# First products of the second and third block on unscaled tiles, residual on one engine, stick scores on all rows

## What is computed

```python
def _rmsnorm(a, gain):
    af = a.astype(jnp.float32)
    af = af * lax.rsqrt(jnp.mean(af * af, axis=-1, keepdims=True) + EPS)
    return (af * gain.astype(jnp.float32)).astype(a.dtype)
...
z = jnp.einsum('bqhd,bkhd->bhqk', qb.astype(jnp.float32), kf) * scale
...
h = rmsnorm_3(x, norm_mix_g[l])
z = h @ w_in[l]
```

## Time and profile before

| | us |
|---|---|
| runs: median of 3 | 2980.92 |
| runs: lowest, highest | 2980.76, 2983.86 |
| the profiled execution | 2986.45 |
| its span | 2984.7 |
| PE, DVE, ACT, POOL busy in it | 2856.8, 1363.2, 1138.4, 1227.8 |

### The profile page before, as it was taken

The page is one execution under the profiler, slowest core; times in us unless marked ns, Lnnn a source line. Parts: engine busy times, 40 slices in busy tenths (PEclk is TensorE's granted clock), DMA queues, the critical chain, the costliest instruction groups (busy, mean ns, idle before and its releaser), DMA issues. The chain is left out here.

```text
span 2984.7 us, 39962 instructions
## 1 busy us (share of the span) xinstructions
PE 2856.8 (96%) x16029; PEld 2324.9 (78%) x16029; DVE 1363.2 (46%) x2463; ACT 1138.4 (38%) x2061; POOL 1227.8 (41%) x590
## 2 busy tenths in 40 slices
PE   6999999999999979999999999999999999999998
PEld 4865558888988867767888989888787767888887
DVE  6336650341132332764553555632477653556620
ACT  4357762222244333333454422222333355422221
POOL 4432224454444532222223545554445423555553
PEclk9999999999999988989999999999999999999999
DMA  7410002223322211112323422223222223422332
GB/s 265 148 50 15 15 29 99 95 96 99 117 90 98 92 50 63 37 42 94 121 76 123 137 85 92 98 98 105 85 85 81 87 74 113 148 90 99 99 99 91
DMA packets 84088, 274.71 MB, mean 92 GB/s; under 512 B 9727, under 2 KB 9983, under 8 KB 83776
## 3 DMA queue, kind: packets, MB, share of 16 engines
q1 hardware_dynamic: 82568, 271.32, 27.6%
q10 hardware_dynamic: 1336, 0.83, 0.1%
HBM read 257.36 MB, written 17.90 MB: 92 GB/s over the span
## 5 line engine op out<-in xcount | busy, mean ns | idle before, releaser
L135 POOL TENSOR_TENSOR weights_lo<-weights_raw,weights_hi 128x1024 fp32r<-128x1024 f32 x413 | 1001.9, 2428 | 1330.4 <-ACT weights_hi L127 1330.4
L127 ACT ACTIVATE weights_hi<-weights_raw 128x1024 fp32r<-128x1024 f32 x413 | 436.3, 1060 | 1055.9 <-PE acc L494 543.4
L492 PE MATMUL acc<-h_hi,weights_hi 128*128 128x512 f32 (+2 forms) x1800 | 663.1, 368 | 25.2 <-POOL h_lo L1374 6.5
L493 PE MATMUL acc<-h_lo,weights_hi 128*128 128x512 f32 (+2 forms) x1800 | 637.5, 354 | 0.0
L494 PE MATMUL acc<-h_hi,weights_lo 128*128 128x512 f32 (+2 forms) x1800 | 637.3, 354 | 0.0
L492 PEld LDWEIGHTS acc<-h_hi,weights_hi 128*128 128x128 f32 x1800 | 344.7, 192 | 106.3 <-issue 53.9
L494 PEld LDWEIGHTS acc<-h_hi,weights_lo 128*128 128x128 f32 x1800 | 344.8, 192 | 46.1
L493 PEld LDWEIGHTS acc<-h_lo,weights_hi 128*128 128x128 f32 x1800 | 345.5, 192 | 40.8 <-issue 0.2
L538 PE MATMUL acc<-weights_hi,h_hi 128*128 128x256 f32 (+2 forms) x448 | 137.2, 306 | 11.9 <-DVE h_lo L1002 5.2
L830 ACT ACTIVATE probs<-probs,low 128x31 f32<-128x31 f32 (+5 forms) x276 | 139.1, 505 | 20.7 <-DVE low L797 20.2
L492 PE MATMUL acc<-y_hi,weights_hi 128*128 128x512 f32 (+1 forms) x384 | 137.9, 359 | 3.1 <-POOL y_lo L1693 2.7
(11 more groups left out here) (437 smaller groups left out, 5285.6 us busy)
## 6 DMA issues: line engine op xcount, KB each, us to landing
weights_raw<-in_stream SPq DMA_DIRECT2D x413, 512.0 KB, 3.3
weight_ring<-in_w_ada SPq DMA_DIRECT2D x24, 512.5 KB, 8.3
gates<-gate_tiles SPq DMA_DIRECT2D x24, 258.0 KB, 4.1
gate<-gates SPq DMA_DIRECT2D x8, 774.0 KB, 5.2
held<-gates SPq DMA_DIRECT2D x8, 768.0 KB, 5.7
gates<-gate_tiles SPq DMA_DIRECT2D x23, 256.0 KB, 4.1
bias_copies<-bias_rows SPq DMA_DIRECT2D x1, 3068.0 KB
table<-bias_copies SPq DMA_DIRECT2D x1, 2560.0 KB, 10.0
```

The costliest lines, as they stand in the source:

```text
L127: act.activation(self.hi[:, at % CUT, :], self.raw[:, at % RAW, :], ACT.Copy).then_inc(self.hi_done, 1)
L135: pool.tensor_tensor(self.lo[:, at % CUT, :], self.raw[:, at % RAW, :], self.hi[:, at % CUT, :].bitcast(F32), ALU.subtract).then_inc(self. ...
L492: pe.matmul(out, left[0], right[0], start=start, stop=False)
L493: pe.matmul(out, left[0], right[1], start=False, stop=False)
```

## The change

At the edge from the first to the second block the residual is added on DVE alone. The normalization behind it also makes unscaled halves of the eight tiles, the low half one tile behind on DVE, and a lane `Led` runs two weight chunks (the stick queries, four units, 32 triples) on these halves into four PSUM banks: 20 triples between the residual's tiles, 7 ahead of the `wide` product and 5 behind it. `ChunkAhead` does the load, the rounding and the low halves of one more chunk ahead of the root. In the second block four more chunks (64 triples) run on the unscaled halves; DVE multiplies their results by the scale as it takes them. `TakeLed` takes the led ones into `alone`, one head to a tile with zeros on the other 64 rows (`Blank`), and `Scaled` is spread on DVE between them. The stick scores then use all 128 rows. At the edge from the second to the third block two chunks (the convolution's values, 16 triples) are led in the same way, two triples ahead of the last sums, four ahead of the `wide` product, ten behind it, without a `ChunkAhead`; two chunks of the recurrence's heads follow on unscaled halves, then the led results are taken, then `Scaled` comes. The three runs become one that is renewed between the blocks with the same end, clearing and barrier. The weights lie in the new order of use.

```diff
@@ Run: one for the three blocks
+    def renew(self):
+        self.close()
+        self.open()
...
@@ new lane: the chunk after the led ones
+class ChunkAhead(Lane):
...
+    def sp(self, sp):
+        self.ws.load(sp, self.first, AHEAD + RAW)
...
+    def act(self, act):
+        self.ws.round(act, self.first, AHEAD)
...
+    def pool(self, pool):
+        self.ws.rest(pool, self.first, AHEAD)
...
+class TakeLed(Lane):
...
+    def dve(self, dve):
+        for u, take in enumerate(self.takes):
+            take(dve, self.acc[:, u]).then_inc(self.taken, 1)
+            yield
...
@@ Norm.dve
-            if self.cut is not None:
-                self.rest(dve, t).then_inc(self.lo_even if t % 2 == 0 else self.lo_odd, 1)
+            if self.cut is not None and t >= self.behind:
+                self.low(dve, t - self.behind)
...
         dve.tensor_scalar(self.root[:, 0], self.sums[0:4, 0:self.quarter], 1.0 / D, EPS, ALU.mult, ALU.add).then_inc(self.mean_done, 1)
+        if self.cut is not None and self.behind:
+            self.low(dve, KT - 1)
...
@@ Residual.dve
             dve.scalar_tensor_tensor(self.source(t), self.source(t), self.gain(t), self.scale, ALU.mult, ALU.mult).then_inc(self.scaled, 1)
-            if t % 2 == 0:
-                self.add(dve, t).then_inc(self.even, 1)
-            yield
-
-    def pool(self, pool):
-        for t in range(KT):
-            if t % 2 == 1:
-                self.add(pool, t).then_inc(self.odd, 1)
+            dve.wait_ge(self.scaled, t + 1)
+            dve.tensor_tensor(self.out(t), self.out(t), self.source(t), ALU.add).then_inc(self.added, 1)
             yield
@@ feed_forward, with a next norm
-                order = spliced(down.slots, [(t + 1) * down.per + 1 for t in range(KT)] + [down.slots] * 2)
-                run.lanes([0] * up.slots + [1 + lane for lane in order], [up, down, norm])
+                led = led_of.open(sem, psum, ws, norm.ready_unscaled)
+                order = [1 + lane for lane in spliced(down.slots, [(t + 1) * down.per + 1 for t in range(KT)])]
+                order += [3] * 2 + [2] + [3] * 4 + [2] + [3] * (led.slots - 6)
+                run.lanes([0] * up.slots + order, [up, down, norm, led])
...
+class Led:
...
+    def open(self, sem, psum, ws, ready):
+        units = [unit for c in range(self.chunks) for unit in feature_units(ws, c, self.source, self.n, self.w, ready=(lambda pe, t: ready(pe, t)) if c == 0 else None)]
+        self.dense = Dense(sem, psum, ws, units, self.chunks, banks=len(units), abreast=len(units), acc=self.acc, lags=self.lags, hold=self.hold)
+        return self.dense
@@ first_block, last phase
+                led_of = Led(lambda t: k.vec[:, gain + t:gain + t + 1], raw, N2, W2, LED2, lead, [1.5, 1.5, 5, 5], 1)
...
-                after = Norm(sem, sbuf, k, A, tiles_of(b.x, N2, W2), T2, N2, W2, added.ready, psum("sums", [P, 512]), psum("wide", [P, N2, 512]), b.scale[:, :])
-                lanes = [dense, cut, norm, added, after]
+                after = Norm(sem, sbuf, k, A, tiles_of(b.x, N2, W2), T2, N2, W2, added.ready, sums, wide, b.scale[:, :], cut=led_of.cut, behind=True)
+                led = led_of.open(sem, psum, ws, lambda pe, t: after.ready_unscaled(pe, t))
+                lanes = [dense, cut, norm, added, after, led, ChunkAhead(ws, led.first)]
...
-                run.lanes(order + [3, 4] * KT + [4] * 2, lanes, 2 * KT)
+                marks = led.marks()
+                tail = [step for t in range(KT) for step in [3, 4] + [5] * len([at for at in marks if t - 1 < at - 0.5 <= t])]
+                left = led.slots - tail.count(5)
+                run.lanes(order[:-1] + [6] + order[-1:] + tail + [4] + [5] * 7 + [4] + [5] * (left - 7), lanes, 2 * KT)
@@ Stick.pe, score
-            rows = slice((head % 2) * HD, (head % 2) * HD + HD)
...
-            pe.matmul(self.scores[0:ROWS2[kb], i % 2, 0:W2], self.fm[rows, SB_K + head // 2, kb * P:kb * P + ROWS2[kb]],
-                      self.qm[rows, SB_Q + head // 2, half * W2:(half + 1) * W2], start=True, stop=True).then_inc(self.scores_ready, 1)
+            pe.matmul(self.scores[0:ROWS2[kb], i % 2, 0:W2], self.fm[:, SB_K + head // 2, kb * P:kb * P + ROWS2[kb]],
+                      self.alone[:, head, half * W2:(half + 1) * W2], start=True, stop=True).then_inc(self.scores_ready, 1)
@@ second_attention, first phase
+            def heads_apart(i, half):
+                def take(dve, acc):
+                    cols = columns_of(half)
+                    dve.tensor_tensor(alone[0:HD, 2 * i, cols], acc[0:HD, 0:w], scale[0:HD, cols], ALU.mult)
+                    return dve.tensor_tensor(alone[HD:P, 2 * i + 1, cols], acc[HD:P, 0:w], scale[HD:P, cols], ALU.mult)
+                return take
+
+            def scaled_tile(dest, i):
+                return lambda dve, half, acc: dve.tensor_tensor(dest[:, i, columns_of(half)], acc, scale[:, columns_of(half)], ALU.mult)
...
-                units = token_units(ws, 0, h, T2, values(SB_V), ready=scaled.ready)
-                for i in range(SP_Q + 2):
-                    units += feature_units(ws, 2 + i, h, n, w, act=tile(qm, i))
...
+                for i in range(2):
+                    units += feature_units(ws, i, lambda t: raw.tile(t, T2), n, w, dve=scaled_tile(qm, SP_Q + i))
+                for i in range(2):
+                    units += feature_units(ws, 2 + i, lambda t: raw.tile(t, T2), n, w, dve=scaled_tile(early, SB_K + i))
...
+                others = [2] + [3] * takes.slots + [1] * scaled.slots
+                begin = 2 * KT
+                span = raw_slots - begin
+                order = [0] * begin
+                for at, lane in enumerate(others):
+                    order += [lane] + [0] * ((at + 1) * span // len(others) - at * span // len(others))
+                run.lanes(order + [0] * (dense.slots - raw_slots), [dense, scaled, apart, takes])
@@ second_block
+        led_of = Led(lambda t: k.vec[:, mix + t:mix + t + 1], next_raw, 1, S, LED3, next_lead, [0, 0], 0)
@@ third_mixer, first phase
-                units = feature_units(ws, 0, h, 1, S, act=tile(value, 0), ready=scaled.ready) + feature_units(ws, 1, h, 1, S, act=tile(value, 1))
...
+                raw_heads = 2
+                units = [unit for i in range(raw_heads) for unit in feature_units(ws, i, lambda t: raw.tile(t, S), 1, S, dve=scaled_tile(hf, i))]
...
+                takes = TakeLed(sem, next_lead, [lambda dve, acc, i=i: dve.tensor_tensor(value[:, i, :], acc, scale, ALU.mult) for i in range(LED3)])
...
-                order = paced((dense.weights, 0, 1), (convolved.weights, 0.16, 1), (decays.weights, 0.3, 0.8))
-                run.lanes([3] * scaled.slots + order, [dense, convolved, decays, scaled])
+                order = paced((dense.weights, 0, 1), (convolved.weights, 0.2, 1), (decays.weights, 0.3, 0.8))
+                run.lanes(order[:raw_slots] + [4] * takes.slots + [3] * scaled.slots + order[raw_slots:], [dense, convolved, decays, scaled, takes])
```

## The result

The changed kernel takes 2991.91 us, median of 6 runs, against 2981.87 for the kernel before: a ratio of 1.004 (95% interval 1.0027 to 1.0053). It is **slower**, by 0.4%: 12 us by the ratio, 10 between the medians. The forecast was 2966, faster by 14.5. The profiled execution took 2995.28, its span is 2993.5.

The account below looks back on a forecast made before the run. TensorE, busy 2856.8 of 2984.7 us (96%), was taken as the bound. Edge 1's 8, edge 2's 0.5 and the scores' 6 sum to 14.5 us off the median of 2980.92, giving 2966; range 2955 to 2977.

Parts of the forecast that it names:

- Everything else: Weight tile order, memory on the other side and renewed blocks, throughout the kernel: counts of barriers and loads unchanged, costing nothing.
- A: The forecast itself, whole kernel: 14.5 us faster, 2966 us, own range 2958 to 2975; chance 0.62.
- Edge 1: First block into second: led products gain 11.8 us, less 3.4 for late takes and 0.5 for low clock; about 8.
- The stalls: Second block's raw phase: three DVE operations beside POOL, standing in front of takes, delay products by 3.4 us, bounds 2 and 5.
- the clock: Edge 1: low clock on the first led triples, which stand among idle time, costs half a microsecond.
- Edge 2: Second block into third: a gain of 4.5 us less 4 us of stall, about +0.5, range -2 to +3.
- both stalls: Edge 2: PE idle 4.8 us at the block end behind a late chunk, then 4 us waiting on Scaled's low halves.
- Scores: Stick stage: 32 scores on 128 rows save up to 0.39 us each, 12.5 in all; half taken, 6.
- D: Rival: DVE bounds both opening phases, loss once its waits exceed 22 us; slower, 2990 us; chance 0.04.
- B: Rival: the stick scores give nothing, so the gain is 8.5 us, 2972.4; chance 0.14.
- C: Rival: edge 2's late chunk and Scaled are hidden, so the gain is 21.5 us, 2959.4; chance 0.12.
- E: Rival: at edge 1 the 20 led triples between residual tiles run late, gaining 7.3 us less, 2973.7; chance 0.08.

Follow-up runs that it names:

- b_before_off: The kernel before, with the normalized halves of the first and third block moved by 32 bytes, tile distance still 2048: 3003.65 us, ratio to before 1.0074.
- j_before_2112: The kernel before, with the first block's normalized halves 2112 bytes apart instead of 2048, start unchanged: 2988.03 us, ratio to before 1.0025.
- l_before_2176: The kernel before, with the first block's normalized halves 2176 bytes apart instead of 2048, start unchanged: 2987.80 us, ratio to before 1.0025.
- e_flat128: The changed kernel, with halves starting on a multiple of 128 bytes and the first block's tiles 2048 bytes apart: 2972.85 us, ratio to before 0.9969.
- k_scaled_dve: h_banks3 with all of Scaled's low halves on DVE, none on POOL: 2955.26 us, ratio to before 0.9917.
- g_scaled_first: e_flat128 with edge 2's two led units run one after the other, and its led takes and Scaled ahead of raw products: 2960.56 us, ratio 0.9933.
- h_banks3: g_scaled_first with three PSUM banks instead of two for dense units of the second block's first phase: 2959.13 us, ratio to before 0.9931.
- i_rows64: h_banks3 with the stick scores reading 64 rows again: 2963.06 us, ratio to before 0.9945.
- the two pairs: a_aligned and h_banks3, each against itself with 64-row scores: 2981.92 against 2989.12 us, and 2959.13 against 2963.06 us.
- a_aligned: The changed kernel with 32 bytes per partition reserved on the right side, so tensors there start on multiples of 64 bytes: 2981.92 us, ratio to before 1.0001.
- f_stride: The changed kernel with halves starting on a multiple of 128 bytes, the first block's tiles still 2112 bytes apart: 2983.32 us, ratio to before 1.0006.

## Why the prediction was wrong

**The step that failed** is the one that costed the rest of the edit: "Everything else (order of weight tiles, memory on the other side, renewed blocks) leaves counts of barriers and loads as they are: nothing." Counts did stay. But the memory on the other side moved the operands of the first and third block's products, and each product became 2 to 3% longer: 344 in 80 us instead of 354. It costs 12.6 us in the first block and 6.9 in the third block's rest. b_before_off, j_before_2112 and l_before_2176 show it in the kernel before, by place alone; e_flat128 takes it out of the change. The work before an edge was taken for unchanged because its code was. With the 19.5 of these two places in it, the forecast's sum would have been -5, a slower kernel; no rival named it. (A's own range, 2958 to 2975, is narrower than its three bounds added up, which give 2954 to 2979; the result lies outside both.)

**With that taken out** (e_flat128), the edit gives 0.31%, 9 us, where 14.5 were forecast. Term by term, from the table:

- *Edge 1*, forecast 8: 108.2 - 106.0 = 2.2 (3.2 in the changed kernel itself, on which the following stands). The stalls were priced well (3.4; one gap of 3.17 and one of 0.54), by the mechanism that was named. The mis-sized term is the clock, 0.5: behind the idle time of the block's end the window from 1100 shows 0.62, behind the gap that from 1128 shows 0.57, together (0.38 + 0.43) x 4 = 3.2 us. And the start was 1.6 later than worked out: when the last add ended (1085.99), eight led triples and the sums of the tile before were still ahead of the last sums on the PE, and not four triples, so these began at 1090.42 - 12.6 = 1077.8 instead of 1076.5. Clock 3.2 - 0.5 = 2.7, start 1.6 and stalls 3.7 - 3.4 = 0.3 make 4.6 of the 4.8 that are missing. Where the clock falls differs from trace to trace: in e_flat128 it is 1.00 behind the same idle time of 1.75 (window from 1091), but 0.50 from 1060 to 1064, among the led products, and from 1116 to 1120, behind the gap. k_scaled_dve, with three banks and no POOL in Scaled, has 108.2 - 99.2 = 9.0, with the full clock in its whole raw phase: the 8 could be reached, in part by luck with the clock.
- *Edge 2*, forecast 0.5: 521.3 - 521.2 = 0.1, in a column that varies by up to 4 between like kernels, so that the nearness says little. But both stalls stood where they were put, and both could be taken away: g_scaled_first gains 10.0 there, h_banks3 and i_rows64, with the same edge, 7.2 and 10.3.
- *Scores*, forecast 6: about 6 by the two pairs, with the price of 0.39 for a score that stands alone; the mechanism was as forecast, but that half of the 12.5 would be paid was a guess between two bounds, and that it fits so closely is luck. The column shows 933.9 - 922.3 = 11.6; the kernel before has 925.0 in this stage in b_before_off, 928.0 in j_before_2112 and 924.6 in l_before_2176, so the profiled execution of before was itself long there. It lost 34.1 us of the clock in the stage, and its window from 1160 to 1400 shows 0.89 beside the 0.95 above:

```profile
1160.00:1400.00 240.00, 228.99 (x1243) 165.51 (x1243) 151.25 (x374) 95.26 (x188) 54.84 (x33) 0.89 0.13 42
```

The page on packing, in the Trainium skill "TensorEngine Tiling (Array Packing)", "Theoretical Speedup", gave the rival to this term, a value of 0. No run here packed two scores, so the page's gain itself is not tested; for scores that stand alone between full-row products the pairs decide, and full rows are the faster ones.

**The rivals.** D ended on the right side for a reason that was not its own: its waits of DVE on POOL are there, but they are 3.7 us of gaps and not 22. B, C and E did not happen: the scores gave their part, edge 2 stood still, and led products ran between the tiles: 12 of the 20 triples had begun when the last add ended, and all 20 were ahead of the last sums.

## What to carry to other kernels

Moving a tensor is an edit of every instruction that reads it. Before a change is costed at nothing, its operands' start and the distance of their tiles are compared with those before, in all code that uses the memory, and a count of products in a window of unbroken PE work shows at once whether they are as fast as they were. An order in which a short operation (a take) stands behind long ones on the same engine is worth an experiment with one more buffer (2.5 us of the stage here, the whole within noise), and a block's end is worth a look for the chunk that is still being prepared.

## What the runs showed that was not expected

The rate of these products of 512 columns at the full clock depends on where the moving operand (the halves, which stream through the PE while the weights stay) lies. Products in 80 us, all other code the same in kind: start on 128 bytes and tiles 2048 apart, 354 or 355 (before, e_flat128); start 64 beyond a multiple of 128, 2048 apart, 351 (a_aligned, third block); start on 128 and 2112 or 2176 apart, 346 or 347 (f_stride, j_before_2112, l_before_2176); start 32 beyond a multiple of 64, 344 (after, b_before_off). The Trainium skill, "SBUF — State Buffer", section "Specifications (TRN2)", tells of lines of 16 bytes and a penalty for each new one. Every start and distance here is a multiple of 16, so by that all would be alike; the measurement decides. All three products of a triple pay: in the first block of the changed kernel each takes 233 ns from its start to the next one's, against 226 or 227 before. Whether the place of the weights counts as well was not tried, and what in the memory makes the difference stays open.
